# Three groups of instructions at new places in a selected attention: two of exponentials in ScalarE's queue, one of scores in TensorE's

## What is computed

```
h = rmsnorm(x) * (1 + sc1) + sh1
proj = h @ w_in                      # hq hf hi hg | sq sk sv | iq ik iw | cu
# selected attention, 4 heads of 64, for each block of 128 queries
score = sum_h w[h] * relu(q_idx[h] . k_idx)      # 8 index heads of 32
score = where(key <= query, score, -1e30)
sel   = top_k(score, 128)                        # the keys that a query sees
p = softmax(q . k[sel] / 8);  o_b = p . v[sel]
# recurrence: f = lb + (1 - lb) sigmoid(hf), q = silu(hq), gate silu(hg)
# convolution: 31 taps over tokens, 256 channels
mix = concat([o_a, o_b, o_c]) @ w_out
```

## Time and profile before

| | us |
|---|---|
| median of 3 runs | 1214.02 |
| lowest and highest of them | 1212.85, 1214.28 |
| the profiled execution, its own time | 1213.32 |
| its span | 1211.5 |
| TensorE busy | 1192.1 |
| VectorE busy | 803.4 |
| ScalarE busy | 689.3 |
| GpSimd busy | 428.9 |

### The profile page before, as it was taken

The page is one execution under the profiler, slowest core; times in us unless marked ns, Lnnn a source line. Parts: engine busy times, 40 slices in busy tenths (PEclk is TensorE's granted clock), DMA queues, the critical chain, the costliest instruction groups (busy, mean ns, idle before and its releaser), DMA issues.

```text
span 1211.5 us, 19747 instructions
## 1 busy us (share of the span) xinstructions
PE 1192.1 (98%) x7198; PEld 967.7 (80%) x7198; DVE 803.4 (66%) x1695; ACT 689.3 (57%) x1337; POOL 428.9 (35%) x260
## 2 busy tenths in 40 slices
PE   9999999999999999999999999999999999999997
PEld 8777777777887777789777777777988889899897
DVE  6766767775777676666689767766671266375575
ACT  6666666675446777734567886754442353443442
POOL 0000000002520000053477788314354477675663
PEclk9999999999999999999999999999999999999999
DMA  5322244442633223342322112323363323323322
GB/s 204 118 70 88 82 145 128 133 140 58 203 119 108 88 87 90 120 146 81 113 70 70 36 54 70 121 68 113 118 204 109 122 70 105 105 84 126 105 70 70
DMA packets 37983, 127.62 MB, mean 105 GB/s; under 512 B 4592, under 2 KB 7280, under 8 KB 37888
## 3 DMA queue, kind: packets, MB, share of 16 engines
q1 hardware_dynamic: 35360, 121.39, 31.2%
q10 hardware_dynamic: 2528, 4.98, 1.3%
HBM read 122.91 MB, written 2.13 MB: 103 GB/s over the span
## 4 chain that ended last, share of the span: by engine, by line
PE 87%; DVE 4%; ACT 3%; issue 3%; DMA 1%; POOL 1%; ACTq 0%; DVEq 0%; SPq 0%; POOLq 0%
PE G L1045 18%; PE G L1047 17%; PE G L1046 17%; PE S L1172 2%; PE O L1233 2%; PE G L2098 2%; PE G L2099 2%; PE G L2100 2%; PE T L1212 1%; PE S L1397 1%; PE T L1444 1%; PE O L1460 1%; PE S L2099 1%; PE S L2100 1%; PE S L2098 1%
## 5 line engine op out<-in xcount | busy, mean ns | idle before, releaser
L612 POOL TENSOR_TENSOR wL<-w,wH 128x1024 fp32r<-128x1024 f32 x89 | 222.2, 2503 | 689.6 <-ACT wH L2253 689.3
L1045 PE MATMUL G<-hi,wH 128*128 128x512 f32 x1032 | 419.6, 407 | 2.0 <-POOL wL L612 1.6
L1047 PE MATMUL G<-hi,wL 128*128 128x512 f32 x1032 | 404.0, 391 | 0.0
L1046 PE MATMUL G<-lo,wH 128*128 128x512 f32 x1032 | 403.7, 391 | 0.0
L1045 PEld LDWEIGHTS G<-hi,wH 128*128 128x128 f32 x1032 | 194.3, 188 | 51.4 <-issue 11.0
L1047 PEld LDWEIGHTS G<-hi,wL 128*128 128x128 f32 x1032 | 194.1, 188 | 42.3
L1046 PEld LDWEIGHTS G<-lo,wH 128*128 128x128 f32 x1032 | 194.6, 189 | 38.2 <-issue 2.2
L2253 ACT ACTIVATE wH<-w 128x1024 fp32r<-128x1024 f32 x140 | 147.6, 1056 | 101.6 <-DMA w<-weights_dram 49.6
L2808 DVE TENSOR_TENSOR wL<-w,wH 128x1024 fp32r<-128x1024 f32 x51 | 62.3, 1221 | 11.3 <-ACT wH L2253 10.5
L1162 DVE CUSTOM_DVE_ANT_0 adaw<-adaw,scr 128x1024 f32<-128x1024 f32 x36 | 62.1, 1724 | 0.0
L1200 ACT ACTIVATE scr<-scr,sa 128x256 f32<-128x256 f32 (+2 forms) x64 | 35.2, 558 | 23.7 <-DVE sa L1187 23.7
(11 more groups left out here) (555 smaller groups left out, 2514.5 us busy)
## 6 DMA issues: line engine op xcount, KB each, us to landing
w<-weights_dram SPq DMA_DIRECT2D x150, 512.0 KB, 3.6
adaw<-ada_dram SPq DMA_DIRECT2D x48, 512.0 KB, 4.4
wp<-weights_dram SPq DMA_DIRECT2D x20, 512.0 KB, 4.4
kd<-c_dram ACTq DMA_DIRECT2D x8, 512.0 KB, 3.6
xT<-x_dram SPq DMA_DIRECT2D x4, 512.0 KB, 7.7
out_dram<-xT SPq DMA_DIRECT2D x8, 256.0 KB, 2.3
scr<-ca_dram SPq DMA_DIRECT2D x2, 512.0 KB, 5.2
kd<-cbias SPq DMA_DIRECT2D x8, 128.0 KB, 4.8
```

Source lines behind the costliest of these rows:

```text
L612: g.tensor_tensor(wL[:, u.slot], raw_home(u), wH[:, u.slot].bitcast(f32), ALU.subtract).then_inc(w_lo, 1)
L1045: mm(home[:, :], whi, H[:, k, :], start=(k == first), stop=False)
L1046: mm(home[:, :], whi, L[:, k, :], start=False, stop=False)
L1047: last = mm(home[:, :], wlo, H[:, k, :], start=False, stop=(k == final))
```

## The change

Three groups of instructions change their places; none is added, taken out or altered.

```
             gemm_i(10)
+            gemm_i(11, (0, 1))
             scores_c(pe, 0)
-            gemm_i(11)
+            gemm_i(11, (2, 3, 4, 5, 6, 7))
             turn_c(pe, 0)
...
                 take_turned_c(act, 1)
+                exps_c(act, 2)
                 forget(0)
                 split_h(1)
-                exps_c(act, 2)
                 terms(CONV_C[1], CONV_C[2])
                 take_turned_c(act, 2)
                 queries(0)
+                exps_c(act, 3)
                 split_h(2)
-                exps_c(act, 3)
                 terms(CONV_C[2], CONV_C[3])
```

## The result

| | before | after |
|---|---|---|
| median of 6 runs each, us | 1214.09 | 1218.4 |
| lowest and highest | 1212.85, 1214.28 | 1217.56, 1219.28 |
| profiled execution, its span | 1213.32, 1211.5 | 1218.89, 1217.1 |

The ratio is 1.0038, with a 95% interval of 1.0026 to 1.0051: the change makes the kernel 4.3 to 4.6 us slower. I had forecast slower, by 2.8 us, with 1217.6 as the upper end of the range. The direction and the meetings of VectorE with GpSimd came as forecast; the size did not, and the median lies 0.8 us above the range.

A forecast was written before the change was run, and what follows sets the result against it. TensorE, busy 1192.1 of 1211.5 us, bounds the kernel, with VectorE tight before the last scores. Of 2.5 us gained 0.5 is left; three meetings make the sum +2.8: 1214.02 + 2.8 = 1216.8 us, range 1213.4 to 1217.6.

The forecast's parts named there:

- meetings of VectorE with GpSimd: VectorE instructions kept out by GpSimd's at line 1059, line 3073 and the mask; forecast with three, +2.8 us, chance 0.64.
- TensorE's own sum: Waits removed on TensorE by the three moves: 0.75 + 0.84 + 0.94 = 2.5 us; last scores reached at 672.04.
- The deciding pair: GpSimd's split at 664.75, 0.14 us ahead of VectorE's line 1059 at 664.89, which takes 2.8 us instead of 0.69: +2.1.
- The second and third meeting: Line 3073 (3074 after the change) meets GpSimd's next split, +3.0; the mask meets an addition, +3.3 to +3.6.
- GpSimd's additions between the two splits: Three additions, one stretched to 1.68 us, two of about 1.1, done by about 670.8, when the next split begins.
- the 3.4 that the sum used: Delay of the banks for the last scores from the meetings: transposes at 675.1 + 3.4 = 678.5 instead of 675.63.
- The step that failed: Last scores' two heads run one after the other once banks come free; transposes follow at 674.0 + 1.06 = 675.1.
- The rivals: Four: -0.5 us (chance 0.12), +0.8 us (0.16), the full gain of 2.5 us (0.04), +4 us (0.04).
- The fourth: Longer waits than worked out, with a fourth meeting in the stretch behind: +4 us, 1218.0, chance 0.04.

The follow-up runs named there:

- the filled kernel: The changed kernel with 20 matmuls whose result nobody reads put into TensorE's wait ahead of the last scores; ratio 1.0027.
- the scores' move alone: The kernel before with only the scores moved behind two tiles; 1216.75 us, ratio 1.0029.
- exponentials of turn 2 alone: The kernel before with only the exponentials of turn 2 moved ahead of the softplus and the split; ratio 1.0023.
- both filled ones: The changed kernel with 42 or with 20 matmuls whose result nobody reads ahead of the last scores; ratios 1.0056 and 1.0027.
- both query products away: The changed kernel with line 1059 a round earlier and `queries_2(0)` moved between the logits of turns 4 and 5; 1214.83 us, ratio 1.0014.
- one operand from PSUM: The changed kernel with line 1059 reading the query unit from its PSUM bank instead of the SBUF copy; ratio 1.0019.
- the free way and the moves: The changed kernel with line 1059 at round 10, `queries_2(0)` behind `logits_c(5)`, fourth split behind the terms, 0.9991; second kernel with one more tile ahead of last scores, 0.9991.
- the query product earlier: The changed kernel with VectorE's line 1059 at round 10 instead of 11; 1215.55 us, ratio 1.0020.
- the control, the free way alone: The kernel before, without the moves, with `queries_2(0)` behind `logits_c(5)` and the fourth split behind the terms; 1212.73 us, ratio 0.9997.

## Why the prediction was right in direction and wrong in size

**TensorE's own sum, 2.5 us: right.** The scores of turn 0 came without a wait (631.46, less the 0.41 that the stretch is late: 631.05, as worked out). Turn 3's stand at 656.06 and turn 4's at 664.28 by the same reckoning, against 656.0 and 664.3. Turn 5's could have begun 0.32 us behind the last matmul ahead of them (672.14): 672.05 by the same reckoning, against 672.04.

**The deciding pair: right.** GpSimd 0.14 us ahead of line 1059, 2.80 us for it, and +2.1 at its end (668.13 - 0.41 - 665.58 = 2.14). The prediction called this the step on which the sign hangs, and moving that one instruction out of the pair, by a round or by an operand, took half of the loss back.

**The second and third meeting: right in kind, somewhat short in size.** Line 3074 ended 3.33 us later where +3.0 stood, and the logits of turn 4 began 3.87 later (676.95 - 0.41 - 672.67) where +3.3 to +3.6 stood. The term that failed is that of GpSimd's additions between the two splits: I had put two of them at about 1.1 us, from another place in the trace, but they took 1.24 and 1.25. The trace of before has these very additions in the same stretch, with that duration:

```profile
667.77 1.24 POOL L647 TENSOR_TENSOR tmp<-tmp,rms 128x491 f32<-128x491 f32 x1
668.98 1.24 POOL L647 TENSOR_TENSOR tmp<-tmp,rinv 128x491 f32<-128x491 f32 x1
```

The next split so begins 0.4 us later than worked out (671.62 - 0.41 = 671.2 against 670.8), and line 3074 is held 0.3 us longer. Together with the mask this is 0.45 us over the 3.4 that the sum used. A shorter row from afar was taken for the one at the place itself.

**The step that failed: what comes behind the wait.** The prediction let the scores' two heads and the transposes follow "674.0 + 1.06 = 675.1", and added the meetings to that. This holds at full clock. It worked out itself that TensorE would stand idle for some four us, and left the durations of what follows as in the earlier trace rows. Measured, the transposes begin 680.32 - 0.41 = 679.9 instead of 678.5: 0.45 us of that are the meetings' and 0.95 the half clock of the scores (2.53 from the scores to the transposes where the filled kernel has 1.58). The transposes and the first matmul behind them lose another 0.95 (1.62 + 0.49 against 0.85 + 0.31). That is 1.9 us in the profiled execution. The sum then reads 2.8 + 0.45 + 1.9 = 5.1; the place says 5.2. In the medians the whole is 4.3 us. The upper end of the range, 1217.6, had room for a longer wait (+3.3) but not for a slower engine behind it.

Should it have been seen? The earlier trace rows show no stretch at half clock, and neither does the trace of before anywhere from 562 to 730 us. But it has one 60 us behind the last scores. The longest of TensorE's waits in that kernel is one of 2.3 us for VectorE, which ends at 737.03 (3.0 us is the sum of two at that line):

```profile
PE T L1874 <- DVE kd L3150: 3.0, 2, 2.3
```

and these are the five us behind it (length; busy time of PE, PEld, DVE, ACT and POOL; granted clock, DMA share, GB/s):

```profile
737.00:742.00 5.00, 4.97 (x22) 4.00 (x23) 3.85 (x10) 4.58 (x10) 3.50 (x4) 0.66 0.10 41
```

0.66 of full speed over 5 us is 1.7 us lost, behind a wait of 2.3 us; the prediction forecast one of some four. So a term was to be had from the kernel before: "the engine stands still, and what does its clock do", nothing to 1.7 us by this stretch, or, from the durations in the earlier trace rows once over (1.06 us for the scores and 0.85 for the transposes, twice as long at half clock), up to +1.9. Either would have put the upper end of the range at about 1219.

**The rivals.** None of them came. The fourth, longer waits, gave +4 us and so nearly the measured number, but by a fourth meeting in the stretch behind, and there nothing more was lost: the 0.41 us from ahead of the stretch and the 5.22 of the place are the whole of the 5.6 by which the span has grown. It would have been right by accident.

## What to carry to other kernels

Where two engines share a way into memory and both are at work by hand-set order, an edit on a third engine that moves either by a few tenths of a microsecond deals the meetings anew. List, for the stretch behind an edit, each VectorE instruction with two SBUF operands beside GpSimd's instructions at their new times, and put such an instruction into a gap, or give it an operand from PSUM, before the waits of a third engine are worked at. And a wait on TensorE can cost its length plus what the work behind it loses at half clock; from two microseconds on, where these traces show it come and stay away, that second part belongs in the range. Look for it in the trace of before, behind the longest wait of the whole kernel and not only in the stretch of the edit.

## What the runs showed of the hardware

**The lock costs the loser a fixed tail.** Line 1059 and line 3074 ended 0.55 us behind GpSimd's instruction at both meetings above, as in the earlier trace rows (0.54 and 0.55), whether they had been kept waiting for two us or for one. Their usual 0.69 us are thus nearly whole still to be done when GpSimd ends. The mask, with one SBUF operand, is kept out as well, but ends only 0.29 (676.91 against 676.62) and 0.28 us (675.67 against 675.39) behind. A lead of 0.14 us was enough for GpSimd, and at the same hundredth (671.80) VectorE was first. The Trainium skill (the same page and section) counts VectorE's operations in a two-port mode among those that take the lock; that the mask takes 0.43 us for 512 elements where the others take 0.69 fits this, and its 2.29 us beside a split agree.

**The half clock and the length of the wait.** Behind the last scores' wait the clock fell to half after 5.3 us and in three of the kernels after 2.6 us. After waits of 2.0 us it fell in one kernel and not in another, and after 2.2 us it did not. Two windows, 675 to 680 us, of the kernels with the scores' move alone and with the exponentials of turn 2 alone, which waited 2.00 and 1.97 us:

```profile
675.00:680.00 5.00, 4.10 (x15) 0.79 0.34 105
```

```profile
675.00:680.00 5.00, 3.61 (x17) 1.00 0.36 105
```

A second wait, for VectorE's line 3150 some 55 us behind the last scores, gives the clearest case. It is 2.34 or 2.35 us long in all thirteen traces, and the half clock came behind it in seven of them (before, the change, both filled ones, both query products away, one operand from PSUM, exponentials of turn 2 alone) and not in the other six. In the two kernels with the free way and the moves it came behind the wait of 0.64 us at 712 us instead. So the length of the wait alone does not decide it; what does, these runs do not settle. The price can be given: 1.6 us (the query product earlier: transposes 0.68 late and the place 2.29) to 1.9 (the change).

**The kernel before has a spread that goes with its clock.** Of its 20 runs beside the first kernels, those with a mean granted clock of 0.999 took 1211.57 to 1212.47 us, those at 0.998 1213.09 to 1213.56, and the two at 0.996 1214.93 and 1215.11: about one us for each thousandth. The traces show one source: the profiled execution of before (0.998, 1213.32 us) has the 1.7 us lost at 737 us, and that of the control, the free way alone (0.999, 1211.80), has none below full clock before TensorE's last matmul. A difference of 0.1% between two kernels of this kind is told only by the medians of many runs, or by where their traces stand at one and the same instruction.
